# Four reorderings in a one-core encoder layer: an O transpose, an O readback, a conv-statistics readback and a ScalarE copy

## The reference

```python
h = rms_norm(x, g_pre_mix)
hc, bg, cg, q, k, v = split(h @ w_in, 6)
y_conv = bg * causal_conv3(cg * hc, w_conv)
scores = q_chunk @ k_band.T * 64**-0.5 + bias          # per head, chunk of 64, band of 576 keys
y_attn = softmax(scores) @ v_band
y = concat(group_rms_norm(y_conv, g_conv_out, 8), group_rms_norm(y_attn, g_attn_out, 8)) @ w_out
x = x + rms_norm(y, g_post_mix)
gate, up = split(rms_norm(x, g_pre_ffn) @ w_ffn_in, 2)
x = x + rms_norm((silu(gate) * up) @ w_ffn_out, g_post_ffn)
```

## Time and profile before

| | |
|---|---|
| median of 3 runs | 1108.85 us (1108.84 to 1109.15) |
| profiled execution, its own time | 1108.85 us |
| profiled execution, span | 1106.8 us |
| TensorE matmul busy | 1096.4 us, 99% |
| TensorE weight load busy | 908.6 us, 82% |
| VectorE (DVE) busy | 764.7 us, 69% |
| ScalarE (ACT) busy | 480.4 us, 43% |
| GpSimd (POOL) busy | 160.4 us, 14% |

### The profile page before, as it was taken

How to read it: one execution, slowest core, us unless ns; L and a number is a source line. 1 busy time by engine, 2 the same in 40 slices (tenths; PEclk the granted TensorE clock), 3 DMA queues, 4 the chain that set the end, 5 groups by cost and what they waited for, 6 DMA issues and landing times.

```text
span 1106.8 us, 16172 instructions
## 1 busy us (share of the span) xinstructions
PE 1096.4 (99%) x5653; PEld 908.6 (82%) x5653; DVE 764.7 (69%) x1267; ACT 480.4 (43%) x911; POOL 160.4 (14%) x258
## 2 busy tenths in 40 slices
PE   8999999999999999999999999999999999999997
PEld 7888887878878888888888888888888888888886
DVE  6878855455656756868777777878787777555584
ACT  6542233666665655734323232323223257444441
POOL 2300022010101220312112211211221110000031
PEclk9999999999999999999999999999999999999999
DMA  7332216300100444535546445543644689677632
GB/s 273 110 119 71 58 57 230 113 20 21 38 2 20 160 163 135 171 96 172 159 145 208 135 123 187 177 146 114 218 136 150 212 304 385 235 232 223 219 115 79
DMA packets 116183, 164.11 MB, mean 148 GB/s; under 512 B 7752, under 2 KB 73304, under 8 KB 116128
## 3 DMA queue, kind: packets, MB, share of 16 engines
q1 hardware_dynamic: 98496, 103.30, 29.2%
q0 software_dynamic: 16464, 55.89, 14.5%
q10 hardware_dynamic: 1168, 4.20, 1.0%
HBM read 119.56 MB, written 46.94 MB: 150 GB/s over the span
## 4 chain that ended last, share of the span: by engine, by line
PE 97%; ACT 1%; DMA 1%; DVE 0%; issue 0%; SPq 0%; DVEq 0%; POOL 0%; POOLq 0%
PE psum L1280 34%; PE psum L1307 18%; PE psum L874 12%; PE psum L1113 10%; PE psum L1164 8%; PE psum L1025 4%; PE psum L917 3%; PE psum L898 2%; PE psum L888 2%; PE psum L863 1%; PE psum L1001 1%; DMA arena<-in_x 1%; PE psum L925 0%; PE psum L1007 0%; PE psum L907 0%; ACT arena L1516 0%
## 5 line engine op out<-in xcount | busy, mean ns | idle before, releaser
L1280 PE MATMUL psum<-arena_r,ws 128*128 128x512 f32 x960 | 224.1, 389 | 0.0
L1280 PEld LDWEIGHTS psum<-arena_r,ws 128*128 128x128 f32 x960 | 180.3, 188 | 37.3
L1280 PE MATMUL psum<-hT,ws 128*128 128x512 f32 x720 | 169.9, 389 | 0.0
L1280 PEld LDWEIGHTS psum<-hT,ws 128*128 128x128 f32 x720 | 135.1, 188 | 27.9
L874 PE MATMUL psum<-hT,ws 128*128 128x512 f32 (+1 forms) x624 | 142.3, 380 | 0.4 <-ACT arena L1542 0.4
L1307 PE MATMUL psum<-hT 128*128 128x512 f32 (+1 forms) x600 | 135.2, 385 | 0.0
L1307 PEld LDWEIGHTS psum<-hT 128*128 128x128 f32 x600 | 111.3, 188 | 22.5
L874 PEld LDWEIGHTS psum<-hT,ws 128*128 128x128 f32 x624 | 107.9, 189 | 20.0 <-issue 0.8
L2401 DVE TENSOR_TENSOR misc<-misc,psum 128x512 f32<-128x512 f32 x100 | 68.4, 684 | 49.1 <-PE psum L1280 45.7
L1724 ACT ACTIVATE ws<-o_raw 128x512 fp32r<-128x512 f32 x40 | 25.1, 627 | 139.2 <-DVE o_raw L2379 138.7
L1164 PE MATMUL psum<-ws,hT 128*128 128x512 f32 x348 | 81.7, 393 | 0.0
(11 more groups left out here) (262 smaller groups left out, 1578.0 us busy)
## 6 DMA issues: line engine op xcount, KB each, us to landing
raw<-in_w_ffn_in SPq DMA_DIRECT2D x44, 512.0 KB, 4.4
act_scratch<-arena POOLq DMA_DIRECT2D x77, 256.0 KB, 3.2
raw<-in_w_in SPq DMA_DIRECT2D x22, 512.0 KB, 3.9
arena<-in_w_ffn_out POOLq DMA_DIRECT2D x22, 512.0 KB, 5.7
arena<-act_scratch SPq DMA_DIRECT2D x38, 256.0 KB, 3.5
arena<-in_x SPq DMA_DIRECT2D x16, 512.0 KB, 6.7
raw<-in_w_out SPq DMA_DIRECT2D x16, 512.0 KB, 3.3
raw<-act_scratch SPq DMA_DIRECT2D x26, 256.0 KB, 3.2
```

What stands on the lines that cost most here:

```text
L1280: last = mm(blocks(bank), w[:, k * P:(k + 1) * P], b_operand(i, part, k), start=fresh_bank and k == 0 and w is hi and part == 0, stop=k == ...
```

## The change

Four places move; no operation is added or taken away.

- TensorE, step (3, 8): `transpose_o(3, PP[1])` moves from before `transpose_p(3, 7)` to behind it. The wait for `biased` moves with it.
- ACT, values stage: `x_copy_even(1)` moves ahead of `copy_v(0)`.
- DVE, front round 4: `conv_stats_read(0)` moves from before `make_u3(4)` to behind `front_low(5, 1)`.
- DVE, attention: `read_o(t, 6)` of pairs 0 to 2 moves from step (t + 1, 0), behind the two `add_bias` calls, to the end of step (t, 8), directly behind `copy_o(t, 6)` and ahead of the `o_eps` operation. For pair 3 it stood there already.

```diff
@@ TensorE, step(t, s)
-                if s == NT and t == LAST:
-                    pe.wait_ge(biased, PAIRS * UNITS)
-                    transpose_o(t, PP[1])
                 if s > 0:
                     pe.wait_ge(exp_done, unit(t, 2 * s))
...
                     transpose_p(t, s - 1)
...
+                    if s == NT and t == LAST:
+                        pe.wait_ge(biased, PAIRS * UNITS)
+                        transpose_o(t, PP[1])
@@ ACT
-            sq_x(2), sq_x(3), high_hT(2), copy_v(0), x_copy_even(1), sq_x(4), copy_v(1)
+            sq_x(2), sq_x(3), high_hT(2), x_copy_even(1), copy_v(0), sq_x(4), copy_v(1)
@@ DVE, front
             front_low(5, 0)
-            conv_stats_read(0)
             make_u3(4)
             front_s(5)
             front_low(5, 1)
+            conv_stats_read(0)
             front_low(5, 2)
@@ DVE, step(t, s), s == 0
                     add_bias(t, 0)
                     add_bias(t, 1)
-                    if t > 0:
-                        read_o(t - 1, NT - 2)
                     return
@@ DVE, step(t, s), s == NT
-                if not more:
-                    read_o(t, NT - 2)
+                read_o(t, NT - 2)
                 chain(stt(o_eps[:, :], lsum[:, :], EPS, lsum[:, :], ALU.mult, ALU.mult))
```

## The result

The changed kernel takes 1117.57 us, the median of 4 runs (1116.72 to 1118.38), against 1108.84 us for the kernel before. The ratio is 1.0079, with a 95% interval of 1.0065 to 1.0091: slower by 8.7 us, where 6.5 were forecast and 1117.3 was the upper end of the range. The profiled execution took 1118.58 us, with a span of 1116.6 us. The four times form two groups, 1116.72 and 1116.89, and 1118.25 and 1118.38. That gap of 1.5 us turns out to be the key.

The account below looks back on a forecast made before the run. TensorE's nearly closed row of matmuls was taken to bound the kernel. The terms 0.92 + 2.0 + 2.7 + 0.87 = 6.49 on 1108.85 gave 1115.3 us (1113.9 to 1116.2), with the range 1112.4 to 1117.3.

Parts of the forecast that it names:

- The rule that TensorE's row is closed: Whole kernel: TensorE has almost no idle time, so every microsecond a reordering makes it stand is added to the end.
- ACT's copy, +0.9: Values stage: x_copy_even(1) ahead of copy_v(0) makes TensorE's products of tile 2 start 0.92 us later.
- read_o, +2.7: Attention, three pair boundaries: read_o waits for the turn back and delays add_bias, costing 1.2, 0.95 and 0.55 us.
- The term of 0.95 at 0 to 1: Boundary of pairs 0 and 1: the later second exponential delays ACT's read_half and TensorE's piece by 0.95 us (0.6 to 1.1).
- transpose_o, +0.9: End of pair 3: the eight transposes leave TensorE's wait and stand on the chain, costing 0.9 us (0.6 to 0.9).
- conv_stats_read, the stall: Front round 4: the later DVE read holds TensorE's stats(1) and product (4, 4) behind it, +2.0 us (1.85 to 2.24).
- The second lateness: norms(0): GpSimd's power and ACT's spread come later too, hidden by about 0.5 us; a slower power shows up to 0.3.
- conv_stats_read, the clock: Behind the stall at stats(1): the sum took stats 1.68 and product 2.90 us, with nothing added for a lower clock.
- rival C: Clock falls to 1.2 GHz for the product behind the stats(1) stall: 2.9 us more, 1118.2; chance 0.04.
- rival D: A second wait behind one of the four places, on a late operand: 1 to 2 us more, 1116.3 to 1117.3; chance 0.07.
- A (cover): One of the two larger terms, conv_stats_read or read_o, is mostly hidden: 1112.6 to 1113.3; chance 0.13.
- B (taken up downstream): The loop from 510 to 890 us absorbs TensorE's delay, so the time stays 1108.85; chance 0.04.

Follow-up runs that it names:

- read_o_only: The kernel before with DVE's read_o(t, 6) alone moved to the end of step (t, 8): 1111.51 us against 1108.82, ratio 1.0025.
- all_filled: The changed kernel with 17 transposes of the identity put before TensorE's wait for conv_var at stats(1): 1115.13 us, ratio 1.0056 to the kernel before.
- all_but_stats: The changed kernel with conv_stats_read(0) back ahead of make_u3(4), so with the other three moves: 1113.22 us, ratio 1.0039 to the kernel before.
- stats_only: The kernel before with conv_stats_read(0) alone moved behind front_low(5, 1): 1112.92 us, ratio 1.0041.
- transpose_only: The kernel before with transpose_o(3) alone moved behind transpose_p(3, 7): 1109.72 us against 1108.82, ratio 1.0008.
- stats_after_sums: The kernel before with conv_stats_read(0) moved behind front_s(5) and ahead of front_low(5, 1): 1111.75 us in three groups, ratio 1.0026.
- stall_dense: The kernel before with an added TensorE wait ahead of product (4, 3) for the second sum of front_s(5): 1113.01 us, ratio 1.0032.

## Why the prediction was wrong, point by point

**The rule that TensorE's row is closed: right.** Every stall of TensorE arrived at the end. Three moves alone add to 4.50 and together to 4.30. In the chains of the two kernels the last run of products takes 204.01 us in both, and starts at 891.04 before and at 900.80 after, the 9.8 by which the spans differ.

**ACT's copy, +0.9: right.** 0.91 in the trace and 0.91 in the times.

**read_o, +2.7: right as a sum.** By the changed trace, from the shift of the rows ahead of and behind each boundary: 0.78 at 0 to 1, 1.20 at 1 to 2, 0.52 at 2 to 3, together 2.5; the times of read_o_only give 2.69. The term of 0.95 at 0 to 1 was 0.17 too large. The second exponential came 1.09 later, not 1.2, and ACT's half copy started 0.10 before the exponential's accumulator had been read, where I had put the two nearly in line.

**transpose_o, +0.9: right.** 0.86 in the trace, 0.90 in the times.

**conv_stats_read, the stall: right.** 1.83 in the chain, at the low end of the 1.85 to 2.24 forecast, 2.0 taken; all_filled lies 1.91 above all_but_stats, which is what this move costs in the times without the low clock. That the matmuls keep their order, which I cited from the Trainium skill, page "TensorE: Matmul & The Clock Gate", section "Step-by-step: what each phase is for", agrees with a row now: product (4, 4), whose operands were made in the round before, did not start before the held stats. The row does not tell the Trainium skill's rule from the wait in TensorE's own program, which holds everything behind it. The second lateness, by the power on GpSimd (3.30 here, 2.94 taken), never showed. The spread behind it ended 3.6 before the norms in the changed kernel, with the low clock's delay as cover, and still 0.35 before them in all_filled.

**conv_stats_read, the clock: this is the step that failed.** The sum let the stats and the product behind the stall run at full clock, 1.68 and 2.90, and put nothing for the low one. The low clock stood in the text as rival C, with a chance of 0.04, and outside the range. The two profiles show the low clock, and the times and mean clocks put a spell into all 4 timed runs of the changed kernel, the 8 further ones of the two groups, and all 5 of stats_only. The price was put at the product alone, 2.9; it was 3.3 in the profiled execution, on the stats too, and in the times 1.5 to 1.8 or 3.1 to 3.3. That rival C's 1118.2 meets the upper group is in part luck: its price was 0.4 too small and the sum under it 0.2 too large. That the lower group lies inside the range is luck as well, since the top of the range was made for rival D, a second wait, which did not occur. Without the clock's part the forecast stands: all_filled, the changed kernel with the idle time filled, takes 1115.13 where 1115.3 was forecast. Where the chance went wrong: I took the absence of a low clock in the kernel before as evidence, while its longest stalls were a quarter of this one and the row that I read, in tenths, could have hidden a short spell. Nor did I look at what follows the stall, 16 matmuls of 2 columns each. The Trainium skill's rule from "Part 1: The HAM clock gate" on the same page, that idleness brings the lower clock, was cited and given too little weight; the trace agrees with it in that the clock was at 0.50 of full speed behind the stall.

**Rivals.** A (cover) did not occur. B (taken up downstream) did not: the loop of `multiply` has no idle time in either kernel. D (a second wait) did not.

**What stays open.** Which stalls let the clock fall, and for how long, is not settled beyond the cases run: by TensorE's idle time, 1.83 before the stats in every run and 1.22 in 7 of 9 runs, 2.32 between dense products in 4 of 6 and 1.58 in 0 of 11, 1.34 at the end of pair 3 never in the 11 runs of transpose_only. Whether light work behind a stall makes the fall likelier is argued from these and not shown. Why one execution has a long spell and the next a short one or none is not shown either.

## What to carry to other kernels

Where TensorE's program is a closed row, the price of a reordering is read from the last wait before the next matmul: who releases it today, by how little, and what is put in front of that releaser. A new stall can have a second price, half of the time for which the clock is down: stalls of 1.22 to 2.32 us had it here in all or most runs of four kernels, and stalls of 0.99 to 1.58 us in three others had none. Put it into the sum with a real chance, the more so where light matmuls stand behind the stall, as far as these runs tell, and look for two or three groups of times. To see a short spell, read the granted clock in stretches of 2 us; the page's tenths hide it. If the lateness can't be avoided, useless transposes in its place can keep the clock up. Here they won 1.5 to 3.3 us, and TensorE started the stats no later than without them (1.85 against 1.83).

## What the runs showed of the hardware that I had not expected

- The clock did not fall in the stalls but after them, with TensorE already at work: during the stats in the changed kernel (at about 153.44, 0.65 behind the stall of 1.83), in the product behind them in stats_only and stats_after_sums, at 150.0 in stall_dense, 0.5 behind its stall. It was back after about 3.4 us, in the changed kernel's profile after 6.8.
- Executions of one program differ by steps of about 1.6 us (1110.17, 1111.7, 1113.4 in stats_after_sums), whereas the kernels without such a spell repeat within 0.1 to 0.8 us.
- The same wait of TensorE for the same DVE read is shown as "issue" in the changed kernel (1.83) and by its releaser in all_filled (0.16 on the weight load). So the label does not say that nothing was waited for.
